# A hybrid encoder layer on one core: second FFN's front partly in the merge, state copies, latents and values issued sooner, the last tile's sums on VectorE

## The reference

```python
h = x + 0.5 * swiglu(rmsnorm(x, ffn1_norm), ffn1_w_gate, ffn1_w_up, ffn1_w_down)      # D_FF = 2816
z = rmsnorm(h, mix_norm) @ w_in            # -> c_q 256 | c_kv 128 | k_rope 32 | u 512 | gate_attn 1024 | gate_ssm 1024
attn = mla(c_q, c_kv, k_rope)              # 8 heads, 64 + 32 query/key dims, 64 value dims, bidirectional
y = s5_forward(u) + s5_backward(u) + D * u # 32 groups of 16 channels, 64 complex states
glu = gelu(y) @ w_glu + b_glu;  ssm = glu[:, :512] * sigmoid(glu[:, 512:])
merged = sigmoid(gate_attn) * (attn @ w_o_attn) + sigmoid(gate_ssm) * (ssm @ w_o_ssm)
h = h + merged @ w_out
h = h + 0.5 * swiglu(rmsnorm(h, ffn2_norm), ffn2_w_gate, ffn2_w_up, ffn2_w_down)
out = rmsnorm(h, final_norm)
```

## Time and profile before

| | |
|---|---|
| median of 3 runs | 2269.32 us (2269.16 to 2269.6) |
| the profiled execution, its own time | 2267.31 us |
| its span in the trace | 2265.5 us |
| PE busy | 2144.2 us, 95% of the span |
| PE weight loads busy | 1779.3 us, 79% |
| DVE busy | 1473.9 us, 65% |
| ACT busy | 916.9 us, 40% |
| POOL busy | 610.1 us, 27% |
| DMA | 263.00 MB, mean 116 GB/s |

### The profile page before, as it was taken

The page is one execution under the profiler, slowest core; times in us unless marked ns, Lnnn a source line. Parts: engine busy times, 40 slices in busy tenths (PEclk is TensorE's granted clock), DMA queues, the critical chain, the costliest instruction groups (busy, mean ns, idle before and its releaser), DMA issues. The chain is left out here.

```text
span 2265.5 us, 27670 instructions
## 1 busy us (share of the span) xinstructions
PE 2144.2 (95%) x10074; PEld 1779.3 (79%) x10074; DVE 1473.9 (65%) x2306; ACT 916.9 (40%) x1552; POOL 610.1 (27%) x510
## 2 busy tenths in 40 slices
PE   5899999999999899999999999899799999999997
PEld 4678888887887798878777887687678888887886
DVE  7786667657777524992447887454766565657777
ACT  5423333323445234225427778422533323324444
POOL 5337777750000003220002333100633333310000
PEclk9999999999999899999999999999899999999999
DMA  3433333349333427331340000362123232349333
GB/s 121 108 90 114 126 118 123 118 160 342 117 98 116 139 80 163 98 89 57 112 140 16 7 7 15 140 234 105 56 88 122 89 121 89 121 142 356 100 96 110
DMA packets 234471, 263.00 MB, mean 116 GB/s; under 512 B 34720, under 2 KB 169376, under 8 KB 233824
## 3 DMA queue, kind: packets, MB, share of 16 engines
q1 hardware_dynamic: 234336, 261.23, 36.4%
HBM read 184.60 MB, written 76.58 MB: 115 GB/s over the span
## 5 line engine op out<-in xcount | busy, mean ns | idle before, releaser
L48 PE MATMUL psum<-f_B_hi,f_A_hi 128*128 128x512 f32 x1232 | 489.8, 398 | 32.2 <-DVE f_A_lo L1036 23.7
L49 PE MATMUL psum<-f_B_lo,f_A_hi 128*128 128x512 f32 x1232 | 484.5, 393 | 0.0
L50 PE MATMUL psum<-f_B_hi,f_A_lo 128*128 128x512 f32 x1232 | 484.2, 393 | 0.0
L48 PEld LDWEIGHTS psum<-f_B_hi,f_A_hi 128*128 128x128 f32 x1232 | 234.2, 190 | 84.9 <-DVE f_A_lo L1036 27.5
L50 PEld LDWEIGHTS psum<-f_B_hi,f_A_lo 128*128 128x128 f32 x1232 | 234.2, 190 | 49.8
L49 PEld LDWEIGHTS psum<-f_B_lo,f_A_hi 128*128 128x128 f32 x1232 | 234.4, 190 | 47.6
L1300 POOL TENSOR_TENSOR f_S<-f_raw 128x512 f32<-128x512 f32 x88 | 134.7, 1531 | 445.5 <-DVE f_A_lo L1036 289.7
L933 ACT CAST f_A_hi<-f_S 128x512 fp32r<-128x512 f32 x176 | 109.2, 623 | 351.5 <-PE psum L50 347.1
L48 PE MATMUL psum<-f_wd,f_hh 128*128 128x512 f32 x616 | 240.4, 390 | 3.6 <-DVE f_wd L1082 3.6
L49 PE MATMUL psum<-f_wd,f_hh 128*128 128x512 f32 x616 | 240.4, 390 | 0.0
L50 PE MATMUL psum<-f_wd,f_hh 128*128 128x512 f32 x616 | 240.2, 390 | 0.0
(11 more groups left out here) (327 smaller groups left out, 4277.3 us busy)
## 6 DMA issues: line engine op xcount, KB each, us to landing
f_h_raw<-hidden SPq DMA_DIRECT2D x154, 256.0 KB, 2.6
hidden<-rows SPq DMA_DIRECT2D x44, 768.0 KB, 4.6
f_raw<-ffn_w_gate SPq DMA_DIRECT2D x44, 512.0 KB, 5.1
f_raw<-ffn_w_up SPq DMA_DIRECT2D x44, 512.0 KB, 5.1
f_wd_raw<-ffn_w_down SPq DMA_DIRECT2D x44, 512.0 KB, 9.2
rows<-x SPq DMA_DIRECT2D x16, 512.0 KB, 7.3
ga_raw<-w_in SPq DMA_DIRECT2D x16, 512.0 KB, 4.3
gates<-ga_sig SPq DMA_DIRECT2D x32, 256.0 KB, 2.2
```

Source lines behind the costliest of these rows:

```text
L48: pe.matmul(out, lhs_hi, rhs_hi, start=first, stop=False, skip_group_check=go_on)
L49: pe.matmul(out, lhs_hi, rhs_lo, start=False, stop=False, skip_group_check=go_on)
L50: return pe.matmul(out, lhs_lo, rhs_hi, start=False, stop=last, skip_group_check=go_on)
```

## The change

Seven edits, all in the order or the engine of work; nothing is computed otherwise.

1. Both FFN fronts: `combine` of the last tile pair (four sums) goes from POOL to DVE, between `sums_low(0)` and `sums_low(1)`; high and low of block (0, 1) come ahead of `sums_high(0)` and `sums_low(0)`.
2. f2's front: the squares of tiles 4 to 6, the stores of tiles 4 to 7 and POOL's weight sums of the first matrix are in the merge; f2 squares tile 7 alone, and one variance and inverse root over four tiles takes the place of two over two tiles.
3. `forward(0)` and `forward(1)` on ACT follow `side.sigmoid(8)` in place of `side.sigmoid(11)`.
4. Latents: 0 and 1 follow the first GLU product, then one behind each, 7 behind the seventh product.
5. Values: the same, behind the wos products.
6. PE's `woa.product(0)` is at the mixer's end, waiting for exp and, k by k, for aT_lo.
7. Semaphores and addresses that these need.

The diff, cut to its core (what is left out hands over the tiles S and stat and the semaphores, and repeats `sooner` on the remaining two engines):

```diff
@@ -979,21 +983,26 @@
             if loaded:
                 high(0, 0)
             lows_high(0)
-            if not loaded:
+            if loaded:
+                square(ST - 1)
+                norm.root(act, 0, slice(QUAD, ST))
+            else:
                 high(0, 0)
-            squares(2)
+                squares(2)
             lows_high(1)
             high(0, 2)
             first_copy(0)
-            squares(3)
+            if not loaded:
+                squares(3)
             high(1, 0)
             high(1, 2)
+            high(0, 1)
             sums_high(0)
             first_copy(1)
             sums_high(1)
             sums_high(2)
             sums_high(3)
-            for q in (1, 3, 4, 5, 6):
+            for q in (3, 4, 5, 6):
                 high(0, q)
             for n in range(MATS):
                 matrix(n)
...
@@ -1063,6 +1072,18 @@
                     q = LOW_BLOCKS[i]
                     dve.wait_ge(s_bhi, low_turned(m, i))
                     dve.tensor_tensor(B_lo[:, q, :, tile(m)], blocks(LOW_BANKS[i][m]), B_hi[:, q, :, tile(m)].bitcast(F32), ALU.subtract).then_inc(s_blo, 1)
+
+            def combine(i):
+                lo_, hi_, t = rows[:, i, :], rows[:, QUAD + i, :], T[i % 2]
+                B11, B21, B12, B22 = lo_[:, 0:HALF], lo_[:, HALF:], hi_[:, 0:HALF], hi_[:, HALF:]
+                dve.wait_ge(s_tr, sum_turned(i - 1, -1))
+                dve.wait_ge(s_xn, QUAD + i + 1 - ahead)
+                dve.tensor_tensor(t[:, 0], B12, B11, ALU.subtract).then_inc(s_T3, 1)
+                dve.tensor_tensor(t[:, 2], B22, B12, ALU.subtract).then_inc(s_T3, 1)
+                dve.wait_ge(s_T3, 1)
+                dve.tensor_tensor(t[:, 1], B22, t[:, 0], ALU.subtract).then_inc(s_T3, 1)
+                dve.wait_ge(s_T3, 3)
+                dve.tensor_tensor(t[:, 3], B21, t[:, 1], ALU.subtract).then_inc(s_T3, 1)
 
             def sums_low(m):
                 for i, q in enumerate(SUM_BLOCKS):
...
@@ -1097,17 +1118,30 @@
             if loaded:
                 low(0, 0)
             lows_low(0)
-            if not loaded:
+            if loaded:
+                dve.wait_ge(s_sq, SQUARES)
+                norm.var(dve, 0, slice(QUAD, ST))
+                norm.inverse(dve, 0, slice(QUAD, ST))
+                scaled(QUAD)
+                scaled(QUAD + 1)
+            else:
                 low(0, 0)
-            normalised(2)
+                normalised(2)
             lows_low(1)
             low(0, 2)
-            normalised(3)
+            if loaded:
+                scaled(QUAD + 2)
+                scaled(QUAD + 3)
+            else:
+                normalised(3)
             low(1, 0)
             low(1, 2)
-            for m in range(QUAD):
+            low(0, 1)
+            sums_low(0)
+            combine(QUAD - 1)
+            for m in range(1, QUAD):
                 sums_low(m)
-            for q in (1, 3, 4, 5, 6):
+            for q in (3, 4, 5, 6):
                 low(0, q)
 
             def matrix(n):
...
@@ -1296,11 +1330,12 @@
                     if n:
                         pool.wait_ge(s_lo, place(n - 1, q) + 1)
                     if i in (1, 3):
-                        pool.wait_ge(s_sum, 4 * n + (1 if i == 1 else 2))
+                        pool.wait_ge(s_sum, sums_done(n, 1 if i == 1 else 2))
                     pool.tensor_tensor(S[:, i], a, b, op).then_inc(s_sum, 1)
 
-            sums(0)
-            for i in range(QUAD):
+            if not loaded:
+                sums(0)
+            for i in range(QUAD - 1):
                 combine(i)
             for n in range(1, MATS):
                 sums(n)
...
@@ -1716,8 +1752,9 @@
                                ACT.Gelu_apprx_tanh).then_inc(s["gelu"], 1)
             for n in range(GATES_FIRST - 1):
                 side.sigmoid(act, n)
-            forward(0)
-            forward(1)
+                if n == GATES_FIRST - 5:
+                    forward(0)
+                    forward(1)
             side.sigmoid(act, GATES_FIRST - 1)
             for b in range(BLOCKS):
                 if b + 2 < BLOCKS:
...
@@ -1866,6 +1903,10 @@
 
             h, qt = g // ST, g % ST
             return (h + 1, PROJECT_AT.index(qt)) if qt in PROJECT_AT and h + 1 < HEADS else None
+
+        def sooner(n):
+
+            return (0, 1) if n == 0 else (n + 1,) if n + 1 < ST else ()
 
         def values_after(g):
...
@@ -2018,12 +2059,14 @@
                 mm.then_inc(s_t, 1)
             for n in range(glu.N):
                 glu.product(pe, n, (lambda k: pe.wait_ge(s_lo, 2 * k + 2)) if n == 0 else None)
-                latent(n)
+                for m in sooner(n):
+                    latent(m)
             for x in range(JOBS):
                 project(0, x)
             for n in range(KT):
                 wos.product(pe, n, (lambda k: pe.wait_ge(s_vlo, k + 1)) if n == 0 else None)
-                value(n)
+                for m in sooner(n):
+                    value(m)
             for g in range(G + LAG + 2):
                 turning = LAG <= g < G + LAG
                 if turning:
...
@@ -2038,6 +2081,8 @@
                         inverses(values_after(g)[0])
                 if g < G and job_after(g):
                     project(*job_after(g))
+            pe.wait_ge(s["exp"], G)
+            woa.product(pe, 0, lambda k: pe.wait_ge(s["av_lo"], 4 * k + 4))
 
         @block.scalar
         def _(act):
...
@@ -2132,12 +2177,12 @@
                 if b:
                     act.wait_ge(glu.read[1], b)
                 act.activation(two(sig[:]), glu.ps[0], ACT.Sigmoid, bias=bias[:, NB + b:NB + b + 1]).then_inc(glu.read[0], 1)
+                latent(2 * b)
+                latent(2 * b + 1)
                 glu.high(act, 2 * b + 3)
                 act.wait_ge(glu.read[1], b + 1)
                 act.copy(sT_hi[:, b, :], val[:, b % 2, :]).then_inc(s_vhi, 1)
                 glu.high(act, 2 * b + 4)
-                latent(2 * b)
-                latent(2 * b + 1)
             for x in range(JOBS):
                 project(0, x)
             for n in range(KT):
...
@@ -2424,12 +2471,16 @@
                     sp.dma_start(gb[:], gain.rearrange("(a d) -> a d", a=1).broadcast_to([P, D])).then_inc(s_gain, 16)
                 if 3 <= u < 7:
                     j, t = (u - 3) // 2, (u - 3) % 2
-                    sp.dma_start(next_raw[j][:, :, t * P:(t + 1) * P], weights[j][:, :, t * PAIRS * P:t * PAIRS * P + P]).then_inc(s_next, 16)
+                    sp.dma_start(next_raw[j][:, :, t * P:(t + 1) * P], weights[j][:, :, t * PAIRS * P:t * PAIRS * P + P]).then_inc(s_next[j], 16)
                 if u == KT + 3:
                     for i in range(QUAD):
                         sp.wait_ge(s_add, i + 1)
                         sp.dma_start(kept[i * P:(i + 1) * P, :], rows[:, i, :]).then_inc(s_store[i], 16)
-            sp.wait_ge(s_next, 64)
+            for i in range(QUAD):
+                sp.wait_ge(s_add, QUAD + i + 1)
+                sp.dma_start(kept[(QUAD + i) * P:(QUAD + i + 1) * P, :], rows[:, QUAD + i, :]).then_inc(s_keep[QUAD + i], 16)
+            for j in range(2):
+                sp.wait_ge(s_next[j], 32)
 
         @block.scalar
         def _(act):
...
@@ -2451,6 +2502,23 @@
                 if u in (KT + 5, KT + 6):
                     i = u - KT - 5
                     norm.root(act, i, slice(2 * i, 2 * i + 2))
+            for m in range(QUAD, ST - 1):
+                act.wait_ge(s_add, m + 1)
+                act.wait_ge(s_sq, m)
+                act.activation(dump[:], rows[:, m, :], ACT.Square, accum_out=next_stat[:, 0, m:m + 1]).then_inc(s_sq, 1)
+
+        @block.gpsimd
+        def _(pool):
+            r = next_raw[0]
+            A11, A21, A12, A22 = r[:, 0:4, 0:P], r[:, 0:4, P:], r[:, 4:8, 0:P], r[:, 4:8, P:]
+            pool.wait_ge(s_next[0], 32)
+            pool.tensor_tensor(next_S[:, 0], A21, A22, ALU.add).then_inc(s_nsum, 1)
+            pool.wait_ge(s_nsum, 1)
+            pool.tensor_tensor(next_S[:, 1], next_S[:, 0], A11, ALU.subtract).then_inc(s_nsum, 1)
+            pool.tensor_tensor(next_S[:, 2], A11, A21, ALU.subtract).then_inc(s_nsum, 1)
+            pool.wait_ge(s_nsum, 2)
+            pool.tensor_tensor(next_S[:, 3], A12, next_S[:, 1], ALU.subtract).then_inc(s_nsum, 1)
+            pool.wait_ge(s_nsum, 4)
 
         @block.vector
         def _(dve):
```

More of the change, by code:

```diff
@@ L701, in ffn_map @@
         where[name], total = base + total, total + size
-    return where, total
+    where["stat"] = base + total
+    return where, total + 5 * ST * 4
 def ffn_phase(nc, tag, gain, w_gate, w_up, w_down, rows, ident, psum, hidden, residual, x=None, finish=None, tables=None, ahead=0, following=None, loaded=None):
@@ L895, in square @@
                     act.wait_ge(s_x[m], 16)
-                if m > ahead:
-                    act.wait_ge(s_sq, m - ahead)
+                if m and not loaded:
+                    act.wait_ge(s_sq, m)
```

(8 more changed lines are left out.)

43 lines of the change are left out of this document (23 added, 20 removed).

## The result

The changed kernel took 2287.84 us (median; 2286.43 to 2289.79), the kernel before 2269.46 us beside it: the ratio is 1.008, with a 95% interval of 1.0066 to 1.0093. It is 18.4 us slower. The profiled execution took 2286.43 us, with a span of 2284.6 us where 2265.5 stood before.

A forecast was written before the change was run, and what follows sets the result against it. PE was taken as the bound, busy 2144.2 of 2265.5 us. Six terms summed to +15.7 on the profiled 2267.3 us, giving 2283.0; 2.0 more for the median gave 2285.0 us, range 2274 to 2292.

The forecast's parts named there:

- Scan, +24.9: Scan: copies behind sigmoid 8 hold ACT until the scan ends, so product 11 starts late; +24.9 us, bounds 20 to 31.
- Latents, -5.4: Mixer: latents turned sooner remove PE's 4.21 us wait for the last latent and some slow clock; -5.4 us.
- Values, -1.5: Mixer: values turned sooner remove the 1.49 us wait of the first scores; -1.5 us, bounds -2 to 0.
- What is late next: Mixer, latents: the next input in line is glu.read, needed only by project(0, 2), 2.7 us later, so the wait goes whole.
- Edit 6, +2.4: Mixer to merge: product 0's lead is lost waiting for the gates tile behind 4 MB of rows; +2.4 us.
- R2: Merge: the gates tile is in time, so edit 6 gives -6.6 us, total +6.7, 2276.0 us; chance 0.12.
- f2's front, -5.2: f2's front: dropping second statistics and a square outweighs sums added to DVE; -5.2 us, bounds -8 to -1.
- R3: f2's front: sums moved to DVE are held by POOL, so the front gains nothing; total +20.9, 2290.2 us; chance 0.15.
- f1's front, +0.5: f1's front: the last pair's sums on DVE use its idle time and a little more; +0.5 us, bounds -1 to +3.
- R1: Scan: the copies do not hold PE, so the kernel is faster; -9.2 us, 2260.1 us; chance 0.03.
- R4: Scan: not shortened and copies no faster, so the stop is deeper; +6.3, total +22, 2291.3 us; chance 0.08.

The follow-up runs named there:

- sums on POOL: The changed kernel with the copies back behind sigmoid(11) and the last pair's sums back on POOL in both fronts: 2258.5 us, ratio 0.9954.
- the copies alone: The kernel before with only forward(0) and forward(1) moved behind sigmoid(8): 2294.85 us, ratio 1.0095.

## Why the prediction was right, step by step

The forecast was 2285.0 us; 2287.8 came, on the side and in the range given. The terms, by the stretches of the table above:

- **Scan, +24.9: measured +24.2**, and +23.9 for the run with the edit alone, 22.9 of it in this stretch. All steps are in the rows, on a clock 1.9 us ahead: scan end 1008.5 (1008.7 forecast), copies until 1015.9 (1016.1), product 11 at 1020.2 (1020.7), wait 26.9 (27.4). Product 11 then took 13.8 us in place of 10.9 (2.9 of slow clock, 2.7 forecast), and the products with C 3.7 in place of 5.4 (1.7, 1.3 forecast): 26.9 + 2.9 - 3.9 - 1.7 = 24.2. The place that the copies hold was right too: one place later frees product 11.
- **Latents, -5.4: -4.4.** The wait of 4.21 went whole. The 1.2 us of slow clock that I took off beside it lie behind the wait, and so in the next stretch: over the 7 us from `project(0, 0)` on the granted clock was 0.79 before and 1.00 after, 1.5 us. Eight traces with the edit have 55.8 to 55.9 us here, five without it 59.7 to 60.3.
- **Values, -1.5: -1.4** in these two traces, 0.8 by the means of all (57.7 without, 57.0 with). That the term came out is luck: the wait of 1.49 went and the 1.5 of clock above came back, but a wait for mx_out took 1.8 of it, 2.6 where 0.9 stood: PE has `value(n)` a product sooner and reaches its next bank before DVE has emptied it. In five of the eight traces with the edit the clock fell at that wait (57.4 to 57.7 us), in three it did not (55.95 to 56.15). "What is late next" was asked of the latents, and not here.
- **Edit 6, +2.4: +2.4.** The step that decides, the tile behind the 4 MB, is shown by taking the 4 MB away: R2's -6.6 is what the edit gives then (6.0).
- **f2's front, -5.2: -2.3**, -3.4 by the means (52.3 in four traces without, 48.8 in five with). This term was mis-sized: PE's product (1, 0) started 4.5 us sooner against the end of the merge (6.8 forecast), and product (0, 1) 1.7 sooner (5.2 forecast). Two steps of it failed, and the clock took a part. The chain was to start some 0.5 us sooner; the first scaling came 13.4 us behind the first of the merge's last four additions, where 13.0 stood, with the clock at the lower level at the turnings ahead of it. In three traces with the edit it was at the upper level there, and the scaling came at 12.2. The first step: the four sums were put at 2.7 us, free; the first two were held to 1.6 and 1.8 by POOL's sums of pair 2, which ran until 1636.7. The second: the scaling of the last two tiles was taken unchanged at 3.58; it took 4.53, since without the second statistics it came earlier against POOL's sums (the first such pair, free, took 2.48). That is R3's mechanism at a part of its strength: of the 6.35 us of statistics about half was kept. (Not each of the six small operations there had been held, as I read it: the reciprocal took 0.17 us, the five others 0.9 to 1.24.) The sums on POOL give 3.3 more.
- **f1's front, +0.5: -1.9.** The product (0, 1) starts at 59.15 where it started at 59.23, so the lists did what I worked out (59.8) within 0.7. The rest I put down to the clock, which was at the lower level for 10.4 us between there and f1's end before, and for 7.0 after: 1.7 us. It scatters: the unchanged f1 ended between 726.4 and 729.4 in four traces, the change's between 727.0 and 728.4 in five. By the means of all traces the two halves of edit 1 cancel at this product: block (0, 1) early gives about 1.3 us, and the sums on DVE cost 1.4.
- **The clock, not in the sum.** The stretch of the attention, the same code in thirteen traces, took 258.8 to 262.5 us. The profile before was the shortest of them, and the only one without a fall of the clock at the value matmuls shown above. That is 2.1 of the 19.1 us, and no edit's.

Sum of the terms as measured: -1.9 + 24.2 - 4.4 - 1.4 + 2.4 - 2.3 = +16.6 where +15.7 was forecast; with the attention's 2.1 and w_out's 0.4 it is the span's 19.1. The errors of single terms were larger than that of the sum: f1 and f2 missed by 2.4 and 2.9 with opposite signs. That they cancelled is luck; the scan term, which is most of the sum, is not.

R1 fell with the copies alone. R4 fell with the scan's length, which got shorter by 6.5 us. R2 needed the queue to be free, and it was not.

## What to carry to other kernels

In an engine's list written by hand, a step that waits for something late stops all that stands behind it. Before it is moved up, list what is queued behind it, and find for each the product that needs it and when; do this for the next one too, with the measured time of the cover. Work that starts sooner on PE is worth what the slowest input of its third or fourth successor allows: look at the DMA queue first, and where a large transfer stands ahead of that input, put it behind before the matmul is moved. Work moved between engines is free where the receiving engine has its own work done before the end is set elsewhere, even if each instruction takes longer there (1.27 us on POOL for 0.68 on DVE).

## What the runs showed of the hardware

**What POOL holds on DVE depends on the operands.** Beside POOL's sums in f2 the low parts that read PSUM kept their pace, 0.61 us each (6.06 for ten, sums on POOL), while in the change those that read two tiles of SBUF took 1.7 in place of 0.65 (3.46 for two), the sums 1.6 to 1.8 in place of 0.68 and the scaling 2.3 in place of 1.24. The Trainium skill, SBUF — State Buffer, section "SBUF: two separate sides", names operations of DVE with two inputs in SBUF among those that take the shared ports; the trace agrees. Operands are not all of it: a TENSOR_SCALAR of 128x2, which reads one tile of SBUF, took 1.24 us beside POOL and 0.17 in the same place of the change. So where its operands lie is the first thing to ask of an operation that is to move to DVE beside POOL, and in the prediction I had the rule for the scan and did not ask it of the sums.

**The clock under the same code.** The same eight value matmuls ran at 0.39 us each in one execution and at 0.63 in another, after equal idle times; the clock fell there in twelve of thirteen traces. A term under 2 us can't be read from one pair of profiles; stretches with the same code in several traces gave the scatter.
